# A depthwise convolution with its shifts in SBUF rows and its channels in column halves, three channel groups on TensorE in layer 0 and two in layer 1, and gated-attention levels set among the gate units

## The reference, cut to what matters

```python
def causal_dwconv(u, w, b):      # w: (31, 512), one filter per channel
    y = lax.conv_general_dilated(u, w[:, None, :], (1,), padding=[(30, 0)], ..., feature_group_count=512)
    return y + b

def token_mixer(h, ...):
    z = h @ w_in                 # q, k, v, g, gate rank, ca, cb
    o = gla_chunked(q, k, v, log_a)                   # gated linear attention, 4 heads
    o = rmsnorm(o, gla_norm_w) * silu(g)
    u = causal_dwconv(ca * sigmoid(cb), conv_w, conv_b)
    u = silu(layernorm(u, cn_w, cn_b))
    return concatenate([o, u]) @ w_out
```

## Time and profile before

| what | value |
|---|---|
| device time, median of 3 runs | 1208.9 us (1208.49 to 1208.99) |
| span of the profiled execution, first to last instruction | 1206.2 us (no device time of its own is given) |
| TensorE busy, share of the span | 99% |
| VectorE, ScalarE, GpSimd busy | 81%, 66%, 4% |
| granted TensorE clock, mean | 0.999 |

### The profile page before, as it was taken

One profiled execution on the slowest core, in us unless ns is written; L12 is line 12 of the kernel. 1 busy time (PEld: TensorE's weight loads), 2 busy tenths in 40 slices (PEclk: granted clock), 3 DMA queues, 4 the chain that ended last, 5 costly groups with the idle time before them and its releaser, 6 DMA issues.

```text
span 1206.2 us, 16760 instructions
## 1 busy us (share of the span) xinstructions
PE 1192.1 (99%) x6775; PEld 1029.6 (85%) x6775; DVE 981.7 (81%) x940; ACT 791.8 (66%) x741; POOL 51.8 (4%) x77
## 2 busy tenths in 40 slices
PE   9999999999999999999999999999999999999997
PEld 8998999999899888888888888888888888888885
DVE  5998755445698979989979879879889989979987
ACT  6865644334566657687677768668668668767764
POOL 5000000000100000000000000000000000000000
PEclk9999999999999999999999999999999999999999
DMA  8942555556555259999999999999999999999990
GB/s 272 368 159 70 192 178 197 185 176 196 187 175 176 73 191 366 381 372 394 376 374 390 376 379 383 377 379 387 381 386 376 381 385 375 380 387 376 395 339 36
DMA packets 182572, 359.61 MB, mean 298 GB/s; under 512 B 9206, under 2 KB 68956, under 8 KB 182492
## 3 DMA queue, kind: packets, MB, share of 16 engines
q1 hardware_dynamic: 178300, 343.28, 79.3%
q0 software_dynamic: 4176, 15.21, 3.3%
q10 hardware_dynamic: 16, 0.00, 0.0%
HBM read 350.60 MB, written 7.86 MB: 297 GB/s over the span
## 4 chain that ended last, share of the span: by engine, by line
PE 94%; DVE 2%; issue 1%; SPq 1%; ACT 1%; DMA 0%; ACTq 0%; DVEq 0%
PE YB L2036 18%; PE WBS L2015 13%; PE WBS L2017 13%; PE WBS L2016 13%; PE YB L1653 6%; PE WBS L1580 5%; PE WBS L1582 4%; PE WBS L1581 4%; PE YB L2027 2%; PE WBS L1767 2%; PE WBS L1614 2%; PE YB L2051 2%; PE WBS L1615 2%; PE WBS L1616 2%; PE YB L1634 1%; PE YB L1797 1%
## 5 line engine op out<-in xcount | busy, mean ns | idle before, releaser
L929 DVE TENSOR_TENSOR w_lo<-raw,w_hi 128x2048 fp32r<-128x2048 f32 x319 | 716.4, 2288 | 85.5 <-ACT w_hi L578 85.2
L578 ACT ACTIVATE w_hi<-raw 128x2048 fp32r<-128x2048 f32 x324 | 598.5, 1915 | 11.0 <-DMA raw<-in_w_in 6.9
L2015 PE MATMUL WBS<-w_hi,t_hi 128*128 128x512 f32 x704 | 278.7, 396 | 0.6 <-DVE w_lo L929 0.5
L2017 PE MATMUL WBS<-w_hi,t_lo 128*128 128x512 f32 x704 | 274.8, 390 | 0.0
L2016 PE MATMUL WBS<-w_lo,t_hi 128*128 128x512 f32 x704 | 274.2, 389 | 0.0
L2015 PEld LDWEIGHTS WBS<-w_hi,t_hi 128*128 128x128 f32 x704 | 132.2, 188 | 29.6 <-issue 2.8
L2017 PEld LDWEIGHTS WBS<-w_hi,t_lo 128*128 128x128 f32 x704 | 132.2, 188 | 28.3
L2016 PEld LDWEIGHTS WBS<-w_lo,t_hi 128*128 128x128 f32 x704 | 132.3, 188 | 26.3
L1580 PE MATMUL WBS<-t_hi,w_lo 128*128 128x256 f32 x448 | 127.2, 284 | 0.0
L1582 PE MATMUL WBS<-t_lo,w_hi 128*128 128x256 f32 x448 | 126.8, 283 | 0.0
L1581 PE MATMUL WBS<-t_hi,w_hi 128*128 128x256 f32 x448 | 126.8, 283 | 0.0
(11 more groups left out here) (315 smaller groups left out, 1384.5 us busy)
## 6 DMA issues: line engine op xcount, KB each, us to landing
raw<-in_we_down SPq DMA_DIRECT2D x88, 1024.0 KB, 7.3
raw<-in_we_gate SPq DMA_DIRECT2D x80, 1024.0 KB, 7.0
raw<-in_we_up SPq DMA_DIRECT2D x80, 1024.0 KB, 6.9
raw<-in_w_in SPq DMA_DIRECT2D x19, 1024.0 KB, 5.6
raw<-in_wd_gate SPq DMA_DIRECT2D x11, 1024.0 KB, 5.3
raw<-in_wd_up SPq DMA_DIRECT2D x11, 1024.0 KB, 5.3
raw<-in_wd_down SPq DMA_DIRECT2D x11, 1024.0 KB, 4.9
raw<-in_w_out SPq DMA_DIRECT2D x8, 1024.0 KB, 11.2
```

Source lines behind the costliest of these rows:

```text
L578: act.activation(w_hi[:, hi_slot(n, item), :], raw[slot][:], ACT.Copy).then_inc(hi_ready, 1)
L929: dve.tensor_tensor(w_lo[slot][:], raw[slot][:], w_hi[:, hi_slot(n, item), :].bitcast(F32), ALU.subtract).then_inc(lo_ready, 1)
L2015: pe.matmul(bank, xs_hi[:, k0 + k, :], hi[:, k, :], start=start, stop=False)
L2017: ins = pe.matmul(bank, xs_lo[:, k0 + k, :], hi[:, k, :], start=False, stop=stop)
```

## The change

The convolution on TensorE takes another form. For a channel group, GpSimd issues 16 DMAs in SBUF that put 32 channels into 32 partitions four times, each time one token further shifted, so that a matmul over 128 partitions applies four taps to 32 channels. The weight has 64 columns (32 channels, and again for taps 16 further on); two matmuls `j` write the two halves of the output's partitions. A group is 2 halves x 4 quads q = 8 steps of two matmuls. In layer 0 three groups (1, 2, 3) are on TensorE, 24 steps, and VectorE has 31 taps of group 0, in two accumulators; in layer 1 two groups (2, 3) are, 16 steps, and VectorE keeps 62. One DMA batch per `conv_input`: in layer 0 for group 1 from `cu`, and in both layers for groups 2 and 3 from `acc`. The weights come from one VectorE instruction for each group (`conv_weights`); layer 1's first is made in the dense stage. ScalarE's `diagonals` and VectorE's `make_pairs` and `pairs` are gone. `place(i)` is four ScalarE instructions of 32 partitions for each group, `add_ahead(i)` four VectorE ones. At the start GpSimd clears `shift_rows` and issues 16 small DMAs ahead of the masks, and TensorE turns `shift_rows` too.

The levels 2 to 7 go between the halves and tiles of CA1, CB1, G0 and G1, and the convolution comes behind them; the lists of ScalarE and VectorE are reordered to suit. The DMA descriptor scratch is set to 4096.

```diff
-    DIAGS = 6
+    APART = 16
+    QS = APART // 4
+    ON_PE = [[1, 2, 3], [2, 3]]
...
+            step(pool.memset(shift_rows[:], 0.0))
+            for l in range(L):
+                for q in range(QS):
+                    for ahead in range(2):
...
+                        pool.dma_start(shift_rows[r0:r0 + 23:2, l, 32 * first:P].rearrange("p (s c) -> p s c", c=32),
+                                       conv_w[l, w0 + first:w0 + 4, P:CH].rearrange("s (b c) -> b s c", c=32)).then_inc(shift_rows_ready, 16)
             step(pool.memset(mask_f[:], 0.0))
...
+                pool.wait_ge(shift_pads, l + 1)
+                if ON_PE[l][0] == 1:
+                    pool.wait_ge(cu_ready, 2 * l + 1)
...
+                            pool.dma_start(shifted[32 * s:32 * (s + 1), b, APART - 1 - s:],
+                                           cu[32 * b:32 * (b + 1), 1, PAD:PAD + n]).then_inc(shifted_ready[0], 16)
+                pool.wait_ge(cu_ready, 2 * (l + 1))
+                for b in range(4):
+                    for s in range(4):
+                        n = T - 3 + s
+                        pool.dma_start(shifted[32 * s:32 * (s + 1), 4 + b:12:4, APART - 1 - s:],
+                                       acc[32 * b:32 * (b + 1), 2:4, 0:n]).then_inc(shifted_ready[1], 16)
...
+                def place(i):
+                    act.wait_ge(conv_grouped, GROUPS_BEFORE[l] + i + 1)
...
+                            act.activation(acc[rows, c, :], conv_bank(l, i)[64 * j:64 * j + 32, T * h_:T * (h_ + 1)], ACT.Identity,
+                                           bias=pv[rows, l, PV_CB + c:PV_CB + c + 1]).then_inc(conv_placed, 1)
...
+            def conv_weights(l, i):
...
+                dve.tensor_tensor(conv_operand(i).rearrange("p q b v j -> p q (b v) j"),
+                                  ident4[:].unsqueeze(1).unsqueeze(1).broadcast_to(shape),
+                                  some.unsqueeze(3).broadcast_to(shape), ALU.mult).then_inc(shift_w_ready, 1)
...
+                            part = acc[rows, c, APART:T]
+                            dve.tensor_tensor(part, part, conv_bank(l, i)[64 * j + 32:64 * j + 64, T * h_:T * (h_ + 1) - APART],
+                                              ALU.add).then_inc(conv_added, 1)
```

VectorE's list in layer 1 (layer 0's ends with conv(2), head_lo, conv(3), add_ahead(1), sum_groups(0), add_ahead(2), sum_groups(1); its add_ahead(0) and conv_weights(0,1), (0,2) come ahead of the head sums, and ScalarE's place(0) ahead of the squares):

```diff
+                    conv(2)
+                    decayed(4)
+                    conv(14)
+                    conv_input(1)
+                    level_read_out(3)
...
+                    decayed(7)
+                    level_read_out(6)
+                    conv_weights(1, 1)
+                    level_read_out(7)
+                    level_read_out(8)
+                    conv(4)
+                    head_sums(0)
+                    head_sums(1)
+                    head_gates()
+                    conv(5)
+                    head_lo(0)
+                    head_lo(1)
+                    conv(7)
+                    add_ahead(0)
+                    sum_groups(0)
+                    add_ahead(1)
+                    sum_groups(1)
```

TensorE:

```diff
+                        for j in range(2):
+                            ins = pe.matmul(conv_bank(l, i)[64 * j:64 * (j + 1), T * h_:T * (h_ + 1)],
+                                            conv_operand(i)[:, q, 2 * h_ + j].rearrange("p v j -> p (v j)"),
+                                            shifted[:, 4 * (c - 1) + 2 * h_ + j, 4 * q:4 * q + T],
+                                            start=(q == 0), stop=(q == QS - 1))
...
+                    level(0)
+                    level(1)
+                    pe.wait_ge(cu_ready, 2 * l + 1)
+                    channels("CA1", between=lambda: level(2))
+                    channels("CB1", between=lambda: level(3))
+                    gates_tile(0, 0)
+                    level(4)
+                    gates_tile(0, 1)
+                    level(5)
+                    gates_tile(1, 0)
+                    level(6)
+                    gates_tile(1, 1)
+                    level(7)
```

and behind that, in layer 0: level(8), conv(8), heads(), conv(11), turn_heads(), conv(5); in layer 1: conv(1), level(8), conv(1), heads(), conv(9), turn_heads(), conv(5). At the start:

```diff
                 pe.wait_ge(rows_ready, 16 * (6 * L + 1))
+                pe.wait_ge(shift_rows_ready, 16 * L * QS * 2)
...
-    nc = bacc.Bacc("TRN2", target_bir_lowering=False, num_devices=1)
+    nc = bacc.Bacc("TRN2", target_bir_lowering=False, num_devices=1, dynamic_dma_scratch_size=4096)
```

More of the change, by code:

```diff
@@ L1177, in mixer @@
-                ins.then_inc(o_gated, 1)
-                conv(4)
-                for g in range(2):
-                    dve.wait_ge(mix_hi, 2 * l + g + 1)
-                    dve.scalar_tensor_tensor(out=t_lo[:, 2 * g:2 * g + 2, :].rearrange("p h t -> p (h t)"),
-                                             in0=WB[g], scalar=pv[:, l, PV_GN:PV_GN + 1],
-                                             in1=t_hi[:, 2 * g:2 * g + 2, :].rearrange("p h t -> p (h t)").bitcast(F32),
-                                             op0=ALU.mult, op1=ALU.subtract).then_inc(mix_lo, 1)
@@ L1196, in mixer @@
-                dve.wait_ge(conv_added, 2 * (l + 1))
-                dve.tensor_tensor(acc_sum[:, 1], acc[:, 2, :], acc[:, 3, :], ALU.add).then_inc(acc_summed, 1)
+                    conv_input(0)
+                    conv(30)
+                    decayed(0)
+                    decayed(1)
+                    differences(2)
+                    differences(3)
+                    lo(b + 7)
+                    decayed(2)
+                    differences(4)
+                    lo(b + 8)
+                    decayed(3)
@@ new lines, in mixer @@
+                    differences(5)
+                    lo(b + 9)
+                    conv(2)
+                    decayed(4)
+                    conv(14)
+                    conv_input(1)
+                    level_read_out(3)
+                    differences(6)
+                    lo(b + 10)
+                    decayed(5)
+                    level_read_out(4)
+                    differences(7)
+                    decayed(6)
+                    lo(b + 11)
+                    level_read_out(5)
@@ L1775, in level, with turn_heads @@
+                def turn_heads():
+                    pe.wait_ge(o_gated, l + 1)
+                    for hd in range(HEADS):
+                        for t in range(TT):
+                            a = HEADS * t + hd
+                            c0 = T * (hd % 2) + P * t
+                            ins = pe.transpose(WB[hd // 2][:, c0:c0 + P], o_sq[:, DV * a:DV * (a + 1)], ident[:])
+                    ins.then_inc(o_turned, 1)
                 def level(n):
+                    if n == 0:
+                        pe.wait_ge(qk_ready, 2 * (l + 1))
@@ L1872, in mixer @@
-                ins.then_inc(o_done, 1)
-                conv(12)
-                pe.wait_ge(o_gated, l + 1)
-                for hd in range(HEADS):
-                    for t in range(TT):
-                        a = HEADS * t + hd
-                        c0 = T * (hd % 2) + P * t
-                        ins = pe.transpose(WB[hd // 2][:, c0:c0 + P], o_sq[:, DV * a:DV * (a + 1)], ident[:])
-                ins.then_inc(o_turned, 1)
-                conv(len(PE_CONV))
+                if l == 0:
+                    level(0)
[11 more added lines that the diff above has]
+                    level(7)
+                    level(8)
+                    conv(8)
+                    heads()
+                    conv(11)
+                    turn_heads()
+                    conv(5)
+                else:
+                    level(0)
+                    level(1)
+                    pe.wait_ge(cu_ready, 2 * l + 1)
+                    channels("CA1", between=lambda: level(2))
+                    channels("CB1", between=lambda: level(3))
+                    gates_tile(0, 0)
+                    level(4)
+                    gates_tile(0, 1)
+                    level(5)
+                    gates_tile(1, 0)
+                    level(6)
+                    gates_tile(1, 1)
+                    level(7)
+                    conv(1)
+                    level(8)
+                    conv(1)
+                    heads()
+                    conv(9)
+                    turn_heads()
+                    conv(5)
```

532 lines of the change are left out of this document (290 added, 242 removed).

## The result

| | before | after |
|---|---|---|
| device time, median of 4 runs each | 1208.7 us (1207.82 to 1208.99) | 1219.34 us (1218.03 to 1220.85) |
| span of the profiled execution | 1206.2 us | 1217.9 us (device time 1219.73) |
| TensorE busy, granted clock | 99%, 0.999 | 98%, 0.995 |

The ratio is 1.009 (95% interval 1.0076 to 1.0105): **0.9% slower**, where 0.5% faster was forecast. The profiled spans differ by 11.7 us, the medians by 10.6.

What follows compares the result with a forecast made beforehand. TensorE's own list was taken to set the end, VectorE close behind. Layer 0 -3.1, layer 1 -3.7, start +0.1, matmul shape changes 0.2: -6.5 us, from 1208.9 to 1202.4; range 1200.5 to 1213, the main case's own 1200.5 to 1205.

Steps and rivals of the forecast that it cites:

- 1, convolution steps: TensorE's convolution: a new step takes 0.45 us; 32 steps become 24 in layer 0 and 16 in layer 1.
- Rival B: TensorE's convolution steps: the column halves run in turn, 0.9 us a step, 1216 us in all; chance 14%.
- 2, levels: Levels 2 to 7, each alone in a unit, cost about 1.03 us each, in sum +0.5 us a layer.
- 3, level 0 to the heads: Mixer stretch before the heads: gains 3.4 us in layer 0, 5.0 in layer 1, where the heads wait some 1.0.
- the 11.6: The us from the heads to the first output unit, held to be dependences that fewer steps don't shorten.
- 4, heads to output: Heads to first output unit: gains 0.2 us in each layer, with waits of 0.2 and about 1.0.
- 5, the new tail: Behind the first output unit: 0.5 us lost in layer 0, 1.5 in layer 1; second sums follow in time.
- 6, shift DMAs: GpSimd's shift transfers: 0.53 us an issue, landing at most 3 us behind the issue's end, hidden in both layers.
- Rival C: GpSimd's queue: slower issues make TensorE wait; gain gone at 0.88 us an issue, 1213 us at 1.0; chance 12%.
- 7, the start: Kernel start: GpSimd's 16 small DMAs, 8.5 us, land hidden by about 14; one more turn costs 0.1 us.
- 8, the rest: conv_weights in the dense stage (1.2 us) lies in VectorE's idle time; padding memsets and scratch size cost nothing.

Runs made afterwards that it cites:

- f_pairs: d_best with levels 2 and 3 together between the halves of CA1, and 4 and 5 together behind the second gate tile: 1204.13 us.
- e_tapall: The changed kernel with tap rows loaded and turned as in the kernel before, all 124 of a layer in one transfer: 1215.9 us.
- c_norows: The changed kernel without the 16 transfers that load shift_rows: 1219.36 us.
- d_best: The changed kernel with stationary tiles at multiples of 128 bytes, tap rows loaded as before, the turn one tile later, VectorE's taps out of the tail: 1203.21 us.
- b_scratch: The kernel before with the descriptor scratch of 4096 and nothing else: 1209.54 us.
- b_pad4: The kernel before with 4 unused floats a partition behind taps and nothing else: 1215.19 us.

## Why the prediction was wrong

- **1, convolution steps: right.** A step of the new form takes 0.45. In the changed kernel, in order of time, eight of them lie between 87.42 and the heads at 91.03, 3.61 us:

```profile
87.42 3.67 PE L1915 MATMUL WBS<-shifted,shift_w 128*64 128x256 f32 x32
```

  Rival B is out. So is, for this pair, the rule cited with it from the Trainium skill ("TensorE: Matmul & The Clock Gate", Part 3), that a weight load overlaps a running matmul only if its row group differs: here the two share all 128 rows and still take 0.45 us together, where one after the other would take 0.9, and over the stretch from level 0 to the heads weight loads are busy 33.73 of the 36.44 us in which TensorE's matmuls never pause.
- **2, levels: mis-sized.** I took 1.03 for a level alone in a unit. Levels 4 and 5 start 4.10 apart (73.12 and 77.22), half of a unit's 5.8 between them, which leaves 1.2. Over six levels that is 1.0 us a layer, most of the shortfall of part 3 (1.2 and 1.4). Two levels side by side pay the change of tile once, not twice (f_pairs). The Trainium skill ("TensorEngine Tiling (Array Packing)", Tiling Modes) says that a change of mode drains TensorE; f_pairs agrees, with 0.34 for each change there and back that it saves.
- **3, level 0 to the heads: right but for part 2.** 2.2 and 3.6 gained against 3.4 and 5.0. The heads' wait in layer 1 is 0.9 (forecast 1.0). Two slips in its working change little: 32.9 and 1.0 make 33.9, not 33.7, and the heads' wait is not the only one in the mixers before, since TensorE also stands 0.3 ahead of each first output unit, which is inside the 11.6.
- **4, heads to output: close.** +0.1 and -0.6 against -0.2 in both, so 0.3 and 0.4 off, with waits for gated o of 0.5 (0.2) and 0.7 (1.0).
- **5, the new tail: mis-sized**, 2.0 and 3.8 against 0.5 and 1.5. The term that I worked out was close: TensorE's wait for the first sums is 0.8 and 1.9, from placements of 0.49 (0.42 forecast) and additions of 0.43 (0.36). The false sentence was "the second sums follow in time". In e_tapall, whose clock is 1.00 there, layer 1's second sums start 2.2 behind the first (1.8 in the kernel before) and the squares 2.5 behind those (1.8), 0.4 of it a wait for ScalarE. Before, two additions (1.34 us) served both groups; now each group has four of its own (1.71 us), and VectorE takes 2.2 us from one sum to the next, where TensorE's list between them takes 1.8. VectorE's w_lo, its centring and ScalarE's squares shift with the sums. That is 1.1 in both layers. The clock takes 0.7 in layer 1.
- **6, shift DMAs: right** in what counts. 0.50 to 0.53 an issue, all batches hidden, no TensorE wait for them. Their landing was not: 3.0 to 5.8 us from the issue, so up to 5.3 behind its end where I had estimated 3 at most. Rival C is out, although the sign that I gave for it showed, a TensorE wait at 16 us that ends on a DMA: the DMA was SyncE's.
- **7, the start: wrong.** I worked out GpSimd's queue, which costs nothing (c_norows), and never costed the rewritten tap_rows load on SyncE's queue, although name its last issue as what TensorE waits for at that turn. In the profiled execution it costs 2.2 us on the queue (1.7 of them in the stretch itself), which with the later landing makes 2.9 of wait, and 1.8 of clock.
- **8, the rest: wrong.** The new sizes of small tiles are in no term of the sum, so they were put at nothing without a reason; they were 7.6 us, the largest term. The scratch size is indeed nothing. No rival held the tiles' place, nor could a count of instructions show it: TensorE's list in these stages is the same.

So parts 1, 3, 4 and 6 came out within 1.5 us each. d_best, in which the three losses are mended, is at 1203.21 where the forecast said 1202.4, but that nearness is partly luck: its two stretches from level 0 to the heads are 2.6 us short of the forecast gain, and its layer 1 from the heads to the experts is 1.5 us better than forecast. What failed is the assumption that the rest of the kernel stays as it is (parts 7 and 8, 12.3 us), and in part 5 the second sums and the clock.

Left open: why 0, 64 and 32 bytes differ; whether the landing of the last small row, 3.2 to 4.4 us in the variants against 2.7 in the kernel before's profile, is more than the traffic of the moment (b_scratch and b_pad4, with the same small rows as before, took 3.5 and 3.6, with 0.5 and 0.8 of wait there); and what decides whether a wait of nearly 3 us costs the clock.

## What to carry to other kernels

When a diff changes the size of any SBUF tile, work out where the stationary tiles behind it now lie, and keep those of hot matmuls at multiples of 128 bytes, the only place that was fast here; compare the mean duration of an untouched group of matmuls first when a stage outside the diff moves. Cost every transfer whose pattern is rewritten by its issue and the issue behind it, on its own queue, and give it a slowest dimension with a large divisor rather than few bytes. Work that is only "behind" an engine's critical instruction is ahead of the next one: put it where that engine waits.

## What the runs showed of the hardware

- A float32r matmul of 512 columns starts each 0.2265 us with its stationary tile at a multiple of 128 bytes, and up to 0.233 at odd multiples of 32, in this kernel, where weight loads lie behind running matmuls. That is 4.8 to 7.5 us in a stage with 960 down matmuls. The recorded weight load is 188 ns in every case; only TensorE's pace changes.
- A DMA of 31 rows of 512 bytes costs SyncE's queue some 0.7 us, and the issue behind it up to 1.4; one of 124 rows 0.5 and 0.3.
- After waits of 2.9 us TensorE's granted clock over 20 to 25 us was 0.66 in two runs and 1.00 in one; after 6.0 it was 0.54, after 2.5 0.50, after 2.2 0.74, after 2.8 in two runs 1.00; after waits of up to 1.6 us at that place it stayed 1.00. In layer 1's tail, with a wait of 1.9, the clock fell in five kernels of ten. At the start it cost 1.8 us (level 0 at 54.59 or 52.83 with the same wait). The Trainium skill ("TensorE: Matmul & The Clock Gate", Part 1: The HAM clock gate) has a wait for a transfer as a cause of the lower level; the runs agree, and add that it isn't certain.
